# Taking the expert choice ahead of the normalised rows: deviation and shift applied behind the matmuls instead of before them

## What is computed

```python
x = layer_norm(ALPHA * x + m @ p['w_o'], p['ln1_g'], p['ln1_b'])
f = moe_ffn(x, ...)
x = layer_norm(ALPHA * x + f, p['ln2_g'], p['ln2_b'])
# inside moe_ffn
scores = sigmoid(t @ w_router)            # 64 experts
biased = scores + router_bias             # 8 groups of 8; 4 groups by their two best, then 8 experts
h = silu(t @ w_gate[e]) * (t @ w_up[e])   # each chosen expert, F = 256
routed = sum over chosen e of weight * (h @ w_down[e])
shared = (silu(t @ ws_gate) * (t @ ws_up)) @ ws_down
```

## Time and profile before

| | us |
|---|---|
| median of 3 executions (829.66 to 831.07) | 829.92 |
| the profiled execution | 829.7 |
| its span, first to last instruction | 828.0 |
| TensorE busy | 811.9 (98%) |
| VectorE busy | 506.6 (61%) |
| ScalarE busy | 195.4 (24%) |
| GpSimd busy | 92.2 (11%) |

### The profile page before, as it was taken

The page is one execution under the profiler, slowest core; times in us unless marked ns, Lnnn a source line. Parts: engine busy times, 40 slices in busy tenths (PEclk is TensorE's granted clock), DMA queues, the critical chain, the costliest instruction groups (busy, mean ns, idle before and its releaser), DMA issues.

```text
span 828.0 us, 12703 instructions
## 1 busy us (share of the span) xinstructions
PE 811.9 (98%) x4523; PEld 509.0 (61%) x4523; DVE 506.6 (61%) x1212; ACT 195.4 (24%) x300; POOL 92.2 (11%) x104
## 2 busy tenths in 40 slices
PE   9999999999999999899999999999999999999994
PEld 7876788888788888544545454444545454454452
DVE  6989899999741367545555454545545454553566
ACT  2210012111221005332222222222222323222225
POOL 1029700000010002100000000000000000000021
PEclk9999999999999999999999999999999999999998
DMA  8432344445489947699999999999999999999971
GB/s 328 154 129 101 127 144 141 148 153 116 157 341 418 394 153 284 209 397 416 421 418 420 420 421 420 419 422 419 422 419 421 420 420 421 419 420 420 418 316 52
DMA packets 50548, 262.03 MB, mean 316 GB/s; under 512 B 10504, under 2 KB 11272, under 8 KB 25296
## 3 DMA queue, kind: packets, MB, share of 16 engines
q1 hardware_dynamic: 45904, 252.88, 76.9%
q0 software_dynamic: 4608, 8.66, 2.8%
HBM read 267.10 MB, written 2.53 MB: 326 GB/s over the span
## 4 chain that ended last, share of the span: by engine, by line
PE 97%; DVE 1%; DMA 1%; ACT 1%; issue 0%; SPq 0%; ACTq 0%; DVEq 0%
PE banks L1209 35%; PE banks L1408 27%; PE banks L1448 14%; PE banks L1381 10%; PE banks L1356 3%; PE banks L1310 1%; PE banks L1224 1%; PE banks L1236 1%; PE banks L1386 1%; PE banks L1423 1%; DMA ring<-w_front 1%; PE banks L1474 0%; ACT cgb L682 0%; PE banks L1316 0%; DVE cgb L1119 0%
## 5 line engine op out<-in xcount | busy, mean ns | idle before, releaser
L1408 PE MATMUL banks<-high,low 128*64 128x512 f32 x848 | 226.1, 592 | 0.2 <-issue 0.2
L1209 PE MATMUL banks<-xT,ring 128*128 128x264 f32 x768 | 176.2, 389 | 0.4 <-DMA ring<-w_front 0.4
L1209 PEld LDWEIGHTS banks<-xT,ring 128*128 128x128 f32 x768 | 144.5, 190 | 30.5 <-issue 5.5
L1408 PEld LDWEIGHTS banks<-high,low 128*64 128x64 f32 x848 | 73.1, 137 | 145.4 <-issue 144.8
L1119 DVE TENSOR_TENSOR cgb<-cgb,banks 128x264 f32<-128x264 f32 x248 | 90.2, 425 | 51.4 <-PE banks L1381 51.4
L1164 DVE SCALAR_TENSOR_TENSOR high<-banks,sml,low 128x1024 f32<-128x1024 f32 x31 | 39.8, 1284 | 122.4 <-ACT low L670 122.4
L1381 PEld LDWEIGHTS banks<-xT,low 128*128 128x128 bf16 x744 | 70.3, 98 | 35.4 <-issue 24.3
L1381 PE MATMUL banks<-xT,low 128*128 128x264 bf16 x744 | 90.2, 276 | 0.0
L516 POOL DMA_INDIRECT low<-x_rows_dram,idx x32 | 31.9, 997 | 428.6 <-DVE idx L1064 407.8
L1408 PE MATMUL banks<-ring,low 128*64 128x512 f32 x176 | 77.4, 592 | 0.0
L1448 PE MATMUL banks<-high,mu 128*64 128x512 f32 x336 | 76.7, 598 | 0.3 <-DVE cgb L1119 0.3
(11 more groups left out here) (295 smaller groups left out, 925.4 us busy)
## 6 DMA issues: line engine op xcount, KB each, us to landing
high<-w_gu SPq DMA_DIRECT2D x108, 1024.0 KB, 23.6
high<-w_dn SPq DMA_DIRECT2D x42, 1024.0 KB, 23.4
ring<-w_front SPq DMA_DIRECT2D x78, 512.0 KB, 3.3
ring<-w_gu SPq DMA_DIRECT2D x22, 1024.0 KB, 25.1
us<-w_dn SPq DMA_DIRECT2D x11, 1024.0 KB, 23.6
bgb<-w_dn SPq DMA_DIRECT2D x6, 1024.0 KB, 21.4
xcb<-w_dn SPq DMA_DIRECT2D x5, 1024.0 KB, 21.7
xT<-x_t SPq DMA_DIRECT2D x4, 264.0 KB, 3.8
```

The costliest lines, as they stand in the source:

```text
L1209: ins = pe.matmul(psum[:, 6 + n % 2, 0:T], ring[:, n % RING, k], rhs[:, k], start=(k == 0), stop=(k == KC - 1))
L1408: ins = pe.matmul(psum[SL * j:SL * j + SL, GU_BANK, :], xg[:, k, SL * j:SL * j + SL], gu[slots[j]][:, k], start=(k == 0), stop=(k == KC - 1))
```

## The change

The kernel after doesn't make x1 at all ahead of the expert choice. DVE and ACT only multiply the centered chunks by the gain (`weighted` = r·g, four chunks each), which needs no s. The logits are still scaled by s, and DVE goes from them straight to the choice. The rows turned and stored are those of r·g; ACT multiplies by s when it copies them from PSUM (s as a column, made by three small matmuls of `dev` with a column of the identity), and adds b when it copies gathered rows into `xg`: eight instructions of 128 columns, one for each chunk, in place of one of 1024. The shared expert's products are made from r·g with b as a 265th column, so `cgb` grows to 265 columns in a chunk; DVE multiplies the product by s and adds the 265th column as shift. `acc` is made by DVE (times ALPHA and s) and ACT (plus ALPHA·b) inside visit 0. The second layer norm writes into `acc`, which is the same buffer as before. Some PSUM banks change places.

```diff
@@ -133,7 +133,8 @@
...
 us = sb("us", [P, KC, T])
-cgb = sb("cgb", [P, KC, T])
+cgb_wide = sb("cgb", [P, KC, T + 1])
+cgb = cgb_wide[:, :, 0:T]
...
@@ -153,6 +154,8 @@
...
 sil, wts = carve(mu[:].rearrange("p a t -> p (a t)"), (FC, T), (TC, E))
+gates = (mu[:, 1], y_flat[:, 0:T])
+dev = mu[:, 0]
...
@@ -187,16 +190,21 @@
...
 meta, dest, gain, row_sum, gain_sum, mean_gain, row_bias = carve(sml[:].rearrange("p a t -> p (a t)"), (2, 2), (2, 1), (2, 1), (2, 1), (1,), (1,), (1,))
-r_, x1, sq = xcb[:], cgb[:], us[:]
-acc = x1
+r_, weighted, sq = xcb[:], cgb, us[:]
+acc = weighted
 POOL_SQUARES = 4
+LOGIT_BANK, BIAS_BANK, COLUMN_BANK = 4, 7, 7
+DVE_WEIGHTED = 4
...
 router_bias = sml[:, 23, 0:1]
+shared_shift = sml[:, 23, 1:1 + 2 * FC]
+dev_column = sml[:, 23, 5:5 + TC]
+acc_shift = sml[:, 23, 8:8 + KC]
...
@@ -413,7 +427,9 @@
...
         sp.dma_start(dn[5], w_dn[1]).then_inc(dn_in[5], 16)
-        sp.wait_ge(x1_scaled, KC)
+        sp.wait_ge(logits_ready, 1)
+        sp.wait_ge(weighted_dve, DVE_WEIGHTED)
+        sp.wait_ge(weighted_act, KC - DVE_WEIGHTED)
...
@@ -461,6 +477,8 @@
...
                            fill=0.0, base=0, channel_multiplier=-1).then_inc(before_ready, 1)
+        pool.wait_ge(s_vec, 16)
+        pool.tensor_copy(cgb_wide[:, :, T], vec[:, V_LN + KC:V_LN + 2 * KC]).then_inc(shift_column, 1)
...
@@ -603,6 +621,9 @@
...
                 act.activation(sq[:, n], src[:, n], ACT.Square).then_inc(squared, 1)
+            if nth == 0:
+                for n in range(DVE_WEIGHTED, KC):
+                    act.activation(weighted[:, n], src[:, n], ACT.Copy, scale=vec[:, V_LN + n:V_LN + n + 1]).then_inc(weighted_act, 1)
...
@@ -610,19 +631,21 @@
...
         act.wait_ge(bias_out, 1)
-        act.activation(router_bias, psum[:, 1, 0:1], ACT.Copy).then_inc(bias_ready, 1)
+        act.activation(router_bias, psum[:, BIAS_BANK, 0:1], ACT.Copy).then_inc(bias_ready, 1)
...
         act.activation(scores_t[:, 0:HT], logits_t, ACT.Sigmoid, bias=router_bias).then_inc(scores_ready, 1)
-        for n in range(KC):
-            act.wait_ge(x1_scaled, n + 1)
-            act.activation(x1[:, n], x1[:, n], ACT.Identity, bias=vec[:, V_LN + KC + n:V_LN + KC + n + 1]).then_inc(x1_ready, 1)
+        act.wait_ge(columns_out, 1)
+        for c in range(TC):
+            act.activation(dev_column[0:tok[c], c:c + 1], psum[0:tok[c], COLUMN_BANK, 256 + c:257 + c], ACT.Copy).then_inc(columns_ready, 1)
+        act.wait_ge(columns_ready, TC)
...
             act.wait_ge(xrow_turned, c + 1)
-            act.activation(xrow[c][0:tok[c]], psum[0:tok[c], 2 * (c % 2):2 * (c % 2) + 2].rearrange("p b f -> p (b f)"), ACT.Copy).then_inc(xrow_ready, 1)
+            act.activation(xrow[c][0:tok[c]], psum[0:tok[c], 2 * (c % 2):2 * (c % 2) + 2].rearrange("p b f -> p (b f)"), ACT.Copy,
+                           scale=dev_column[0:tok[c], c:c + 1]).then_inc(xrow_ready, 1)
+        act.activation(acc_shift, vec[:, V_LN + KC:V_LN + 2 * KC], ACT.Copy, scale=ALPHA)
...
@@ -631,16 +654,13 @@
...
             act.wait_ge(turned, it)
-            act.activation(xg.rearrange("p (b k) s -> p b (k s)", b=2), psum[:, 2:4], ACT.Copy).then_inc(xg_ready, 1)
+            for k in range(KC):
+                act.activation(xg[:, k], psum[:, 2 + k // 4, (k % 4) * P:(k % 4) * P + P], ACT.Identity, bias=vec[:, V_LN + KC + k:V_LN + KC + k + 1]).then_inc(xg_ready, 1)
...
         for f in range(FC):
-            act.wait_ge(shared_gu, f + 1)
-            act.activation(sil[:, f], psum[:, SHARED_BANKS[f], 0:T], ACT.Silu).then_inc(shared_silu, 1)
-        act.wait_ge(shared_gu, 2 * FC)
-        act.wait_ge(x1_ready, KC)
-        for n in range(KC):
-            act.activation(acc[:, n], x1[:, n], ACT.Copy, scale=ALPHA).then_inc(acc_ready, 1)
+            act.wait_ge(gates_scaled, f + 1)
+            act.activation(gates[f], gates[f], ACT.Silu, bias=shared_shift[:, f:f + 1]).then_inc(shared_silu, 1)
...
@@ -654,6 +674,10 @@
...
                 rows_in(it + 2)
+            if first:
+                for n in range(KC):
+                    act.wait_ge(acc_scaled, n + 1)
+                    act.activation(acc[:, n], acc[:, n], ACT.Identity, bias=acc_shift[:, n:n + 1]).then_inc(acc_ready, 1)
...
@@ -995,17 +1019,25 @@
...
             center(0, r_, n)
+        def weight_rows(first, end):
+            for n in range(first, end):
+                dve.wait_ge(centered, n + 1)
+                dve.tensor_scalar(weighted[:, n], r_[:, n], vec[:, V_LN + n:V_LN + n + 1], None, ALU.mult).then_inc(weighted_dve, 1)
+        weight_rows(0, 2)
...
         dve.sem_inc(bank_free[(STRIPS - 1) % 2], 1)
+        weight_rows(2, DVE_WEIGHTED)
         deviation(0)
+        dve.sem_inc(dev_ready, 1)
...
             rows = slice(E * half, E * half + E)
-            dve.tensor_tensor(logits_t[rows], psum[rows, 0, 0:HT], mu[rows, 0, tokens], ALU.mult).then_inc(logits_scaled, 1)
-        for n in range(KC):
-            dve.scalar_tensor_tensor(x1[:, n], r_[:, n], vec[:, V_LN + n:V_LN + n + 1], mu[:, 0], ALU.mult, ALU.mult).then_inc(x1_scaled, 1)
+            dve.tensor_tensor(logits_t[rows], psum[rows, LOGIT_BANK, 0:HT], dev[rows, tokens], ALU.mult).then_inc(logits_scaled, 1)
...
@@ -1105,10 +1137,23 @@
...
                 dve.tensor_reduce(meta[h, u, 0:1], psum[h, 6, 3 * j:3 * j + 3], AX.X, ALU.add).then_inc(weights_read, 1)
+        def scale_shared(f, out):
+            dve.wait_ge(shared_gu, f + 1)
+            st.did(dve.tensor_copy(shared_shift[:, f:f + 1], psum[:, SHARED_BANKS[f], T:T + 1]))
+            st.did(dve.tensor_tensor(out, psum[:, SHARED_BANKS[f], 0:T], dev, ALU.mult))
+        dve.wait_ge(rows_stored, 16 * TC)
+        for f in range(FC):
+            scale_shared(f, gates[f])
+        st.settle()
+        dve.sem_inc(gates_scaled, FC)
+        for f in range(FC):
+            scale_shared(FC + f, hT[:, f])
+        st.settle()
...
             dve.wait_ge(shared_silu, f + 1)
-            dve.wait_ge(shared_gu, FC + f + 1)
-            dve.tensor_tensor(hT[:, f], sil[:, f], psum[:, SHARED_BANKS[FC + f], 0:T], ALU.mult).then_inc(shared_h, 1)
+            dve.scalar_tensor_tensor(hT[:, f], hT[:, f], shared_shift[:, FC + f:FC + f + 1], gates[f], ALU.add, ALU.mult).then_inc(shared_h, 1)
...
@@ -1139,6 +1184,11 @@
...
                 do(dve.tensor_scalar(mean_gain, gain[:, u], -1.0 / D, None, ALU.mult))
+            if before is None:
+                for n in range(KC):
+                    dve.scalar_tensor_tensor(acc[:, n], weighted[:, n], ALPHA, dev, ALU.mult, ALU.mult).then_inc(acc_scaled, 1)
+                dve.wait_ge(acc_scaled, KC)
...
@@ -1307,31 +1357,39 @@
...
             for k in range(first, end):
-                ins = pe.matmul(psum[:, SHARED_BANKS[f], 0:T], gu[3][:, k, f * P:f * P + P], x1[:, k], start=(k == 0), stop=(k == KC - 1))
+                ins = pe.matmul(psum[:, SHARED_BANKS[f], 0:T + 1], gu[3][:, k, f * P:f * P + P], cgb_wide[:, k], start=(k == 0), stop=(k == KC - 1))
...
         def turn_x1(c, k):
-            return pe.transpose(psum[0:tok[c], 2 * (c % 2) + k // 4, (k % 4) * P:(k % 4) * P + P], x1[:, k, c * P:c * P + tok[c]], ident[:])
-        keep_warm(6, 2)
+            return pe.transpose(psum[0:tok[c], 2 * (c % 2) + k // 4, (k % 4) * P:(k % 4) * P + P], weighted[:, k, c * P:c * P + tok[c]], ident[:])
+        def turn_block(c):
+            for k in range(KC):
+                ins = turn_x1(c, k)
+            ins.then_inc(xrow_turned, 1)
+        pe.wait_ge(weighted_dve, DVE_WEIGHTED)
+        pe.wait_ge(weighted_act, KC - DVE_WEIGHTED)
+        turn_block(0)
+        pe.wait_ge(bias_ready, 1)
+        pe.wait_ge(dev_ready, 1)
+        for c in range(TC):
+            ins = pe.matmul(psum[0:tok[c], COLUMN_BANK, 256 + c:257 + c], dev[:, c * P:c * P + tok[c]], ident[:, 0:1], start=True, stop=True)
+        ins.then_inc(columns_out, 1)
         turn_scores()
+        turn_block(1)
...
             pe.wait_ge(gu_in[3][h], 16)
-        for k in range(KC):
-            pe.wait_ge(x1_ready, k + 1)
-            for c in range(2):
-                ins = turn_x1(c, k)
-                if k == KC - 1:
-                    ins.then_inc(xrow_turned, 1)
-            shared_in(0, k, k + 1)
+        pe.wait_ge(shift_column, 1)
+        pe.wait_ge(columns_ready, TC)
+        shared_in(0, 0, KC)
+        pe.wait_ge(xrow_ready, 1)
+        turn_block(2)
         shared_in(1, 0, HC)
-        pe.wait_ge(xrow_ready, 1)
-        for k in range(KC):
-            ins = turn_x1(2, k)
-        ins.then_inc(xrow_turned, 1)
...
@@ -1400,8 +1458,11 @@
...
-            pe.wait_ge(xg_ready, it + 1)
+            if before is not None:
+                pe.wait_ge(xg_ready, it * KC + KC)
             for k in range(KC):
+                if before is None:
+                    pe.wait_ge(xg_ready, k + 1)
```

(7 more changed lines are left out.)

13 lines of the change are left out of this document (9 added, 4 removed).

## The result

The changed kernel took 831.67 us (median of 22 runs, 830.02 to 832.69), the kernel before, run beside it, 830.09 us (22 runs, 829.40 to 831.23). The ratio is 1.0015, with a 95% interval of 1.0009 to 1.0021. The forecast was 828.6 us with a range to 830.0: wrong in sign and outside the range. The 22 times of the changed kernel lie in two groups: nine from 830.02 to 830.79, then 831.21 and 831.44, and eleven from 831.90 to 832.69. Each run also has a mean granted clock of TensorE: in seven of the eleven it is 0.994 or 0.995, in all the others 0.996 to 0.998. The profiled execution, 832.01 us with a span of 829.8, is one of the seven. The mean is a rough sign: in the last 4.0 to 7.1 us of the profiled executions the clock is at its lower level anyway, so 0.995 or less says that it fell once more, 0.997 or more that it didn't, and 0.996 can be either.

What follows compares the result with a forecast made beforehand. TensorE was taken to bound the kernel almost throughout. Terms −1.8 + 0.35 + 0.1 − 0.2 = −1.5, with 0.2 for lateness −1.3 us, gave a median of 828.6 us, range 827.3 to 830.0.

Steps and rivals of the forecast that it cites:

- the choice: Ahead of visit 0: DVE starts the expert choice at 322.25 instead of 324.04, 1.8 us earlier (1.5 to 2.1).
- The eight copies of `rows_in`: On ACT in each visit: eight 128-column instructions at 0.26 us a step, 2.2 us in all, 3.0 at most.
- The slow rival: Eight `rows_in` copies don't end before the next L1408; 31 visits lose 0.35 us each; 839.5 us, chance 8%.
- the 0.35 us: Charge in visit 1 (0 to 0.8) because ACT's shifts in visit 0 make L670 2.0 us late.
- The 0.1 us for the end: Charge at the final store (0 to 0.4), whose pieces are half as long.
- Issued early, it moves as soon as the queue is empty, by 333.0, and frees POOL near 334.7: Before the gather: the last store of rows, issued near 328.6, releases POOL near 334.7 instead of 335.68.
- If the store lands no earlier: Upper bound at the gather: TensorE turns rows at 339.4 to 340.3, losing 0.9 of the 1.8 us.
- The estimate of 2.0 us: Skill's fixed DMA part: last store counts as stored at 335.0, making the sum 0.2 us worse.
- an idle TensorE of over 1 us ahead of the turned rows: Sign before visit 0 that the forecast is wrong because of the store.
- All of it arrives: Rival: column matmuls cost 0.2 us, visit 0's ACT and DVE work fits; −1.9 to −2.2 us, 827.9, chance 24%.
- my own case: The forecast itself, from the choice to the end: −1.3 us, 828.6, its own range 828.1 to 829.1, chance 50%.
- the choice moves, visit 0 doesn't follow: Rival: store lands no earlier or DVE's visit 0 work isn't covered; 0.9 us lost, −0.4, 829.5, chance 18%.

Runs made afterwards that it cites:

- the first experiment: The changed kernel with the 1 MB load of dn[7] issued behind the three stores of rows, not ahead of them: 829.29 us, ratio 0.9991.
- the two fills: Changed kernel with shared products moved ahead of the wait for gathered rows: 831.50 us; the same with the dn[7] load behind the stores: 830.08 us.
- ACT's queue: The changed kernel with the three stores of rows issued by ACT on its own DMA queue, behind its copies: 830.21 us, ratio 0.9999.

## Why the prediction was wrong

**Right: the choice.** 1.75 us earlier for 1.8 forecast. Its terms: the column matmuls took 0.63 us (taken 0.5). The two gain multiplications were in the way of the last centering: it could have started at 315.24, behind the strip's end at 315.20, and started at 315.53, so they cost 0.29 us and not 0.1. Some luck is in the sum, as the strips ended 0.11 us earlier in this execution.

**Right: the prices of the new work.** The eight copies of `rows_in` took 2.17 us (forecast 2.2; the page of the Trainium skill named in the prediction, "ScalarE: Activation LUTs", section "What ACT_TABLE_LOAD costs", gave an estimate of 2.4, and here the measurement decides for the rows). The slow rival, which wanted over 3.5, is out: a steady visit still takes 14.41 us. The rule set beside it is one for operands read from SBUF, and these copies read PSUM. The new making of `acc` took 2.83 us (2.8), and the shifts 3.38 (3.4).

**A charge that wasn't due, and one that was.** L694 came 1.6 us behind its time (L670's 356.57 plus the 1.93 us of the shift is 358.50; it started at 360.12), forecast 2.0. But L1217 ended at 364.99, before TensorE took up the combination at 365.26. From the first matmul of visit 1 to that of visit 2 are 14.41 us as before, so the 0.35 us weren't due. Visit 0 itself takes 0.08 us longer (12.88 against 12.80). The 0.1 us for the end was due: from the last visit's first matmul to the end of the span are 31.44 us against 31.25, and the last stores land in 2.3 us instead of 2.1.

**The step that failed** is "Issued early, it moves as soon as the queue is empty, by 333.0, and frees POOL near 334.7". POOL was freed at 336.84, 2.1 us later. The upper bound beside it, "If the store lands no earlier", was no bound: the store landed 1.2 us *later* than when it was issued 2.5 us later. I let the same loads take the same time in either case. What the runs showed in its place: stores issued early behind loads in the same queue slow the loads down (270 and 213 GB/s against 410 and 389), and held back or moved past 1 MB of load they land 1.0 or 2.1 us earlier. Why the stores slow the loads was not taken further. One reading beneath that step was off too: the last packet of the stores ended at 334.32 in the kernel before, not by 334, so it took 1.36 us to release POOL, not 1.7; in ten of the 14 profiled executions that stretch is 1.36 to 1.39 us. The estimate of 2.0 us beside it is for the whole fixed part of a DMA; here the measurement decides. A bound on a transfer that is moved past others has to be open above as well.

**The term that was missing** is the clock. I had written of "an idle TensorE of over 1 us ahead of the turned rows" as a sign, but priced it by its length alone and gave a fallen clock no chance. In the changed kernel the rows come 1.3 us later than before (340.69 against 339.37). Without the clock visit 0 would start 3.3 us behind them, as with nine filler matmuls (341.14 to 344.41), at 344.0 instead of 343.56: 0.4 us slower. It started at 345.41: the other 1.4 us are the clock. The times say the same: the nine lower runs have a median of 830.41, 0.3 us above the kernel before, the eleven upper ones 832.24, and the seven lowest mean clocks are all among the latter. The Trainium skill's page "TensorE: Matmul & The Clock Gate", section "Part 1: The HAM clock gate (the "warmup" mystery)", says that the throttled level is the default, that activity releases it, and that the count of slow matmuls varies from run to run; that runs of one kernel fall on both sides agrees with it. A forecast should have carried a gap of this size as a case of its own. The two parts don't explain all: of the eleven upper runs one has a mean clock of 0.997 and three of 0.996.

**What would have been right.** "All of it arrives" and my own case needed the store to follow; "the choice moves, visit 0 doesn't follow" had the mechanism, at 829.5, but neither the delay nor the clock. With one load moved the forecast's sum nearly comes out: the first experiment's span is 826.9, 1.1 us under 828.0 (forecast 1.3), and its median 0.8 us under the kernel before.

## To carry to other kernels

Moving a chain forward moves what feeds it from DRAM only if the stores in between land earlier, so look at what lies ahead of them in the queue and put loads that nobody needs soon behind them, but not so many that they meet the transfer that reads the rows back (1 MB paid here, 3 MB cost). A new idle gap of TensorE costs its length and, in a part of the executions, more in clock (1.4 us here, and 1.7 us in visit 0 of the two fills: 14.56 against 12.88); read the granted clock just behind it. And a group of products isn't free filler: it may cover work that the profile's busy rows don't show, such as the sequencer's register loads, and where it is taken away, a gap opens. Where the releaser that a row names was done long before, look for another.

## What was not expected of the hardware

- A small store issued earlier landed later: 328.90 to 336.84 against 331.43 to 335.68, and the engines' rate fell to 213 GB/s beside it, with load packets of 0.54 us instead of 0.31.
- The granted clock fell to 0.50 behind idle times of 2.76 us, and behind pairs of short ones as well (1.07 and 1.41 us; 1.40 us alone with the load moved), in some executions of a kernel and, by the mean clock, not in others. With 1.82 us (stores held) and 1.39 us (ACT's queue) no run's mean clock went under 0.996 (the profiled ones kept 1.00), and with 2.84 us (stores held, the load behind them) the profiled execution kept 1.00. The length of the gap alone doesn't decide it; what does is open.
- An indirect gather of 128 rows took 3.7 to 3.9 us on idle DMA engines and 7.44 us beside loads at 401 to 442 GB/s.
- Two register loads of TensorE's sequencer and what goes with them took 1.6 us up to the next matmul, in both runs in which nothing ran beside them.
- Why stores that were held until no load was moving any more landed 2.4 us later than unheld ones, and why single executions of a kernel spread by 1 us and more at the same mean clock (TensorE's waits for weights vary from 0.2 to 2.1 us between profiles), stays open.
